# Norm roots by square root and reciprocal instead of logarithm and exponential, and an earlier place for two scalings of the final norm

## The reference

```python
def rmsnorm(x, g):
    xf = x.astype(F32)
    y = xf * lax.rsqrt(jnp.mean(xf * xf, axis=-1, keepdims=True) + EPS)
    return (y * g.astype(F32)).astype(x.dtype)
...
hs = modulate(rmsnorm(xs, norm2_g[l]), m_lat[3], m_lat[4])
xs = xs + m_lat[5] * swiglu(hs, w_ffn_in[l], w_ffn_out[l])
...
y_sample = rmsnorm(xs, final_g)
```

## Time and profile before

| | us |
|---|---|
| median of three runs | 2845.01 |
| profiled execution, its own time | 2845.1 |
| its span | 2843.3 |
| TensorE matmuls busy in the span | 2721.0 (96%) |
| VectorE busy | 1798.9 (63%) |
| ScalarE busy | 884.6 (31%) |
| GpSimd busy | 871.4 (31%) |

### The profile page before, as it was taken

How to read it: one execution, slowest core, us unless ns; L and a number is a source line. 1 busy time by engine, 2 the same in 40 slices (tenths; PEclk the granted TensorE clock), 3 DMA queues, 4 the chain that set the end, 5 groups by cost and what they waited for, 6 DMA issues and landing times. The chain is left out here.

```text
span 2843.3 us, 41885 instructions
## 1 busy us (share of the span) xinstructions
PE 2721.0 (96%) x16344; PEld 2595.5 (91%) x16344; DVE 1798.9 (63%) x2662; ACT 884.6 (31%) x1454; POOL 871.4 (31%) x392
## 2 busy tenths in 40 slices
PE   7998888999999999999999998899999999999998
PEld 5997777999999999999899997559999999999997
DVE  6798986755666666666658614545466666666665
ACT  4213666251122222221542231542512222222214
POOL 0673123422222222222412121434322222222223
PEclk9999999999999999999999999999999999999999
DMA  6543101500111111110335434323101111111102
GB/s 251 182 149 97 18 21 42 204 30 31 45 44 44 44 44 44 44 44 30 124 116 185 169 122 178 130 82 139 45 30 45 44 44 44 44 44 44 44 30 82
DMA packets 64072, 227.29 MB, mean 80 GB/s; under 512 B 8080, under 2 KB 18768, under 8 KB 58576
## 3 DMA queue, kind: packets, MB, share of 16 engines
q1 hardware_dynamic: 62368, 225.12, 22.8%
q10 hardware_dynamic: 1584, 0.51, 0.1%
HBM read 191.52 MB, written 29.88 MB: 78 GB/s over the span
## 5 line engine op out<-in xcount | busy, mean ns | idle before, releaser
L1538 DVE SCALAR_TENSOR_TENSOR x<-ps,mod,x 128x384 f32<-128x384 f32 (+2 forms) x944 | 493.6, 541 | 397.2 <-PE ps L222 397.2
L220 PE MATMUL ps<-hh,wi_hi 128*128 128x384 f32 x2112 | 708.6, 336 | 8.2 <-ACT hid L1132 4.5
L222 PE MATMUL ps<-hh,wi_lo 128*128 128x384 f32 x2112 | 706.2, 334 | 0.0
L221 PE MATMUL ps<-hl,wi_hi 128*128 128x384 f32 x2112 | 706.1, 334 | 0.0
L1294 POOL TENSOR_TENSOR wi_lo<-raw_in,wi_hi 128x1024 fp32r<-128x1024 f32 x80 | 197.7, 2471 | 1016.8 <-ACT wi_hi L1113 1016.8
L220 PEld LDWEIGHTS ps<-hh,wi_hi 128*128 128x128 f32 x2112 | 396.9, 188 | 10.9 <-ACT hid L1132 5.2
L221 PEld LDWEIGHTS ps<-hl,wi_hi 128*128 128x128 f32 x2112 | 397.1, 188 | 0.8
L222 PEld LDWEIGHTS ps<-hh,wi_lo 128*128 128x128 f32 x2112 | 396.9, 188 | 0.0
L220 PE MATMUL ps<-fac_hi,wo_hi 128*128 128x384 f32 x656 | 221.0, 337 | 4.0 <-DVE x L1538 3.2
L1113 ACT ACTIVATE wi_hi<-raw_in 128x1024 fp32r<-128x1024 f32 x80 | 84.7, 1059 | 444.2 <-PE ps L222 444.2
L222 PE MATMUL ps<-fac_hi,wo_lo 128*128 128x384 f32 x656 | 219.9, 335 | 0.0
(11 more groups left out here) (325 smaller groups left out, 5679.6 us busy)
## 6 DMA issues: line engine op xcount, KB each, us to landing
raw_in<-in_w_ffn_in_dram SPq DMA_DIRECT2D x80, 512.0 KB, 3.6
wmt<-in_w_mod_t_dram SPq DMA_DIRECT2D x56, 512.0 KB, 3.6
wo_raw<-in_w_ffn_out_dram SPq DMA_DIRECT2D x22, 1024.0 KB, 4.8
gla_spill<-turn SPq DMA_DIRECT2D x22, 576.0 KB, 3.7
oraw<-in_w_in_odd_dram SPq DMA_DIRECT2D x24, 512.0 KB, 5.2
wmt_odd<-in_w_mod_t_dram SPq DMA_DIRECT2D x24, 512.0 KB, 4.3
x<-in_x_dram SPq DMA_DIRECT2D x8, 1152.0 KB, 9.9
wm<-in_w_mod_dram SPq DMA_DIRECT2D x16, 512.0 KB, 11.8
```

Source lines behind the costliest of these rows:

```text
L220: pe.matmul(acc, w_hi, in_hi, start=first, stop=False, skip_group_check=resumed)
L221: pe.matmul(acc, w_hi, in_lo, start=False, stop=False, skip_group_check=resumed)
L222: return pe.matmul(acc, w_lo, in_hi, start=False, stop=last, skip_group_check=resumed)
L1538: last = dve.scalar_tensor_tensor(out=x[:, ft, cols], in0=ps[:, bank, loc], scalar=mod[:, layer, GATE2 * KT + ft, v:v + 1], in1=x[:, ft, c ...
```

## The change

`logarithm` and `power` go. In their place `root` first runs `warm`, an activation of one column with the square root as its function, that waits for nothing and whose result (in `silu_c`) nobody reads; then `square_root` with the same bank, bias and scale as the logarithm had, which posts `rooting`. The reciprocal of `stat` is made by VectorE in `invert`, at the head of the third's first `scale` or `scale_final`: it waits for `rooting`, takes the reciprocal of 128x384 in place, posts `rooted`, and waits for its own post. TensorE's waits for `logged` become waits for `rooting`. This holds for the three thirds of all four seams, twelve roots. The very first norm of the kernel keeps its logarithm and exponential.

In the final norm `root` of third 1 stands where its `logarithm` stood, with the reciprocal on VectorE ahead of the third's scalings. Six `scale_final` of third 0 instead of four stand ahead of the last gate; the other two come behind `plain_low(5)` and behind the first two adds of third 1.

```diff
         def root(self, act, c, bank):
-            self.logarithm(act, c, bank)
-            self.power(act, c)
-
-        def logarithm(self, act, c, bank):
+            self.warm(act, 3 * (self.n - 1) + c)
+            self.square_root(act, c, bank)
+
+        def square_root(self, act, c, bank):
             act.wait_ge(self.averaged, c + 1)
-            act.activation(self.stat[:, c], bank, ACT.Ln, bias=eps[:], scale=1.0 / D).then_inc(self.logged, 1)
-
-        def power(self, act, c):
-            act.wait_ge(self.logged, c + 1)
-            act.activation(self.stat[:, c], self.stat[:, c], ACT.Exp, scale=-0.5).then_inc(self.rooted, 1)
+            act.activation(self.stat[:, c], bank, ACT.Sqrt, bias=eps[:], scale=1.0 / D).then_inc(self.rooting, 1)
+
+        def warm(self, act, j):
+
+            act.activation(silu_c[:, j // 2, j % 2:j % 2 + 1], ones[:, 0:1], ACT.Sqrt)
+
+        def invert(self, dve, c):
+            dve.wait_ge(self.rooting, c + 1)
+            dve.reciprocal(self.stat[:, c], self.stat[:, c]).then_inc(self.rooted, 1)
+            dve.wait_ge(self.rooted, c + 1)
 
         def scale(self, dve, c, kk):
             if kk == 0:
-                dve.wait_ge(self.rooted, c + 1)
+                self.invert(dve, c)
...
         def scale_final(self, dve, c, kk):
             if kk == 0:
-                dve.wait_ge(self.rooted, c + 1)
+                self.invert(dve, c)
...
-                tail.logarithm(act, 1, end_bank[1])
+                tail.root(act, 1, end_bank[1])
                 for ft in range(6, KT):
                     square_final(2, ft)
-                tail.power(act, 1)
                 tail.root(act, 2, end_bank[2])
...
-                for kk in range(4):
+                for kk in range(6):
                     tail.scale_final(dve, 0, kk)
                 gate(L, 5, 1, 2, 11)
                 plain_low(5)
-                plain_add(1, range(0, 4))
-                for kk in range(4, KT):
-                    tail.scale_final(dve, 0, kk)
-                    plain_add(1, range(kk, kk + 1))
+                tail.scale_final(dve, 0, 6)
+                plain_add(1, range(0, 2))
+                tail.scale_final(dve, 0, 7)
+                plain_add(1, range(2, KT))
                 plain_add(2)
```

More of the change, by code:

```diff
@@ L235, in __init__ @@
             self.squared, self.summed, self.averaged = sem("squared"), sem("summed"), sem("averaged")
-            self.logged, self.rooted = sem("logged"), sem("rooted")
+            self.rooting, self.rooted = sem("rooting"), sem("rooted")
             self.scaled, self.high, self.low = sem("scaled"), sem("high"), sem("low")
@@ L613, in first_pair @@
                     if c == 0:
-                        pe.wait_ge(self.norm.logged, 2)
+                        pe.wait_ge(self.norm.rooting, 2)
                     for m in range(2):
@@ L619, in first_pair @@
                         if c == 2 and m == 1:
-                            pe.wait_ge(self.norm.logged, 3)
+                            pe.wait_ge(self.norm.rooting, 3)
                         block(m, c)
@@ L1476, in _ @@
                 pe.wait_ge(win_low, 2)
-                pe.wait_ge(norm.logged, 1)
+                pe.wait_ge(norm.rooting, 1)
                 pe.wait_ge(taken, place[LAST, 1] + 1)
@@ L1484, in _ @@
                 pe.wait_ge(win_low, 4)
-                pe.wait_ge(norm.logged, 2)
+                pe.wait_ge(norm.rooting, 2)
                 pe.wait_ge(taken, place[LAST, 2] + 1)
@@ L1505, in _ @@
                     hidden(L, n, order=last_blocks)
-                pe.wait_ge(tail.logged, 1)
+                pe.wait_ge(tail.rooting, 1)
                 contract(1)
@@ L2155, in opening @@
             rows_done, rows_out, mod_done, modulated = sem("rows_done"), sem("rows_out"), sem("mod_done"), sem("modulated")
-            squared, summed, averaged, logged, rooted = (sem("squared"), sem("summed"), sem("averaged"), sem("logged"),
+            squared, summed, averaged, logged, rooted = (sem("squared"), sem("summed"), sem("averaged"), sem("rooting"),
                                                          sem("rooted"))
```

## The result

The changed kernel takes 2851.18 us at the median of 15 runs (2846.55 to 2855.51), against 2845.12 us for 15 runs of the kernel before on the same chip. The ratio, from all these runs, is 1.0017 with a 95% interval of 1.0010 to 1.0024: 4.8 us slower, between 2.8 and 6.8 (the two medians by themselves lie 6.1 us apart). The prediction was 2848.8, a sum of +3.8. The slowdown itself is outside the noise; whether it is more or less than 0.2% the interval doesn't tell.

What follows compares the result with a forecast made beforehand. TensorE's matmuls bound the kernel (96% of the span), so only its waits and the tail count. Mid seams +1.8, end of layer 0 -0.2, final norm +2.2 gave +3.8 us: 2848.8 us, range 2842.5 to 2854.5.

Steps and rivals of the forecast that it cites:

- the likeliest case alone: Whole kernel: with a reciprocal of 2.2 to 2.66 us, the time spans 2846.5 to 2850.5 us.
- The reciprocal: On VectorE, 384 columns: taken as 2.45 us, between 2.36 and 2.64 extrapolated from rows of one and nine columns.
- second rival: The reciprocal takes 3.2 us in the same chains: +10.5 us, 2855.6, slower; chance 0.26 with all reciprocals above 2.66.
- the first: First rival: the reciprocal streams in 0.55 us, -7.5 us in all, 2837.6; chance 0.15 with other unseen gains.
- The root in its place: Each root, ScalarE free to first scaling: 0.73 us longer with a table load, 0.57 shorter without.
- fourth rival: Square root's table does not stay; squares, copies or high parts force loads: some +8 us, 2853; chance 0.06.
- Mid seams: Both mid seams: TensorE's restart at the second gate moves 0.89 us later in each, +1.8 us together.
- the wait at third 0's last parts: Mid seams: a new TensorE wait of 0.3 us, absorbed in the 0.44 it waited at the first gate.
- third rival: Mid seams take up the 0.9 and only the tail pays: 2847.1 us, no change; chance within the forecast's 0.53.
- End of layer 0: VectorE's add comes 0.31 us later, TensorE's 0.5 us wait for GpSimd's split goes: -0.2 us in sum.
- Final norm: Third 1 scaled 0.2 us earlier, third 2's reciprocal in VectorE's list between scalings adds 2.4: +2.2 us.
- 9R - 18.3: Whole kernel's change in us, with R the reciprocal's time: nothing at 2.03, +5.5 at 2.64.

Runs made afterwards that it cites:

- e4: The change with the reciprocal reading 64 columns of ones instead of 384 and the square root scaled by a constant; 0.9976 of the kernel before.
- e5: The change with only third 2 of the final norm back on logarithm and exponential, scaling order kept; 1.0006 of the kernel before.
- e8: The change with one Abs_reciprocal_sqrt activation replacing square root and reciprocal, and no warm activation; 2836.35 us, 0.9970 of the kernel before.
- e9: The kernel before with eight one-column ScalarE copies, results unread, ahead of root 2 in each mid seam; 1.0002 of the kernel before.
- e12: The kernel of e9 executed once more, against the kernel before; 2848.57 us in one run.

## Why the prediction came out right

The verdict it gave, no change within 0.2% and leaning slower, holds by the ratio, with 3.8 us predicted and 4.8 [2.8, 6.8] measured; the interval reaches past 0.2%. The median of 2851.18 lies in the stated range and above the 2850.5 that the likeliest case alone was to reach. Step by step:

- **The reciprocal**: 2.45 predicted, 2.55 measured, inside the middle bounds 2.36 and 2.64. Nine columns against one gave the right slope (5.75 and 6.5 ns per column around 6.25) although 384 is forty times as far. The Trainium skill, "VectorE: DVE Perf Modes", section "First, the fixed hardware budget", has a repeat count of 8 for it, from which the prediction estimated 3.2 us; the trace has 2.55, and the measurement decides. With it the second rival falls, and with e4 in hand the first.
- **The root in its place**: 0.84 longer with a load (5.13 - 4.29 to the first scaling, and 4.61 - 3.77 for third 2), which is 2.55 - 1.72 = 0.83. The loads are those that were counted, so the fourth rival is out.
- **Mid seams**: +0.89 each predicted, 3 x 2.55 - 6.46 = +1.2 with the measured reciprocal; +1.39 and +0.89 measured. In layer 0 one step was wrong: the wait at third 0's last parts was to be absorbed in the first gate's. With two more behind it (at 597.30 and 597.96), it delays TensorE's own sum for third 1 (598.83 - 581.62 = 17.21 us behind the mark, before 596.31 - 579.87 = 16.44), and ScalarE, which used to spend that time on a load, now stands 0.18 us before the square root for it (the first row of ScalarE's fence above). The delay passes on through the root: 0.84 - 0.47 + 0.18 + 0.84 = 1.39, the four terms being root 0, root 1 without a load, this wait and root 2. In layer 1 the predicted 0.89 came out by luck. There the first scaling of third 0 meets an add of GpSimd, in the kernel before and in the change:

```profile
2007.89 1.01 POOL L263 TENSOR_TENSOR stat_mid<-stat_mid,sq_mid 128x384 f32<-128x384 f32 x1
2008.00 1.05 DVE L292 SCALAR_TENSOR_TENSOR hl_f<-x,amod,stat_mid 128x128 f32<-128x128 f32 x1 [4.32 <-ACT stat_mid L285]
...
2011.50 1.02 POOL L263 TENSOR_TENSOR stat_mid<-stat_mid,sq_mid 128x384 f32<-128x384 f32 x1
2012.15 0.53 DVE L297 SCALAR_TENSOR_TENSOR hl_f<-x,amod,stat_mid 128x128 f32<-128x128 f32 x1
```

In layer 0, where no add of GpSimd runs beside it, that scaling lasts 0.35 in both kernels. In layer 1 it lasts 1.05 before and 0.53 in the change, where it starts later against the add. That takes up 0.52 of root 0's delay, third 1 is scaled 21.56 us behind the mark instead of 21.52, and the 0.89 is in the main root 2: 0.84 - 0.52 - 0.47 + 0.20 + 0.84 = 0.89, the 0.20 being ScalarE's wait for the sum there. That the add is what stretches the scaling is read from the times alone; no run tried it. The third rival, that the seams absorb the delay, is out for the sum of both, though layer 1 absorbs a part.

- **End of layer 0**: the add's wait grew by 0.33 (0.31 predicted), and the split's wait went. -0.60 measured for -0.2: the gain was undersized, since it was priced at the wait's idle time alone. From TensorE's two matmuls with ones ahead of the split's wait to the second start behind it are 1421.13 - 1419.52 = 1.61 us before and 1423.71 - 1422.89 = 0.82 after, 0.79 less, where 0.52 is idle time.
- **Final norm**: +2.44 for +2.2, and 2 x 2.55 - 2.7 = 2.4 by its own formula. Third 1's scaling comes 0.14 earlier (0.2 predicted), the scalings meet the gate within 0.02 us, and the reciprocal in VectorE's list costs what it lasts. e5 shows that this root is all of it.

With 2.55 the formula 9R - 18.3 gives +4.7; the stages add up to +4.1. The end of layer 0 (0.5 too high) and the second mid seam (0.3 too high) outweigh the first (0.2 too low). That the forecast of +3.8 lies closer to 4.1 than this is luck: a reciprocal taken 0.1 too short lowered the sum by 0.9. What the prediction did not see is that a version with the same eight loads and no reciprocal was there to be had. The Trainium skill, "ScalarE: Activation LUTs", section "What it computes", advises, because of accuracy, VectorE's reciprocal and a `Sqrt` activation in place of the `Rsqrt` function, which was not tried here; the change has these two in the other order. e8's function is another one, and in these chains it is some 13 us ahead of the change's pair by the two ratios (1.0017 [1.0010, 1.0024] and 0.9970 [0.9958, 0.9982]). Times say nothing of how exact either is.

## What to carry to other kernels

Swapping a table load for an operation on another engine is priced at each place by itself: here one edit in twelve roots gained where the old load stood in the way of a later activation, lost 0.8 us where it stood in the chain, and lost the operation's whole length where the old work had been hidden behind the very engine that got the new one. Price an unseen size of an operation from two sizes of the same operation, not from a copy of the right shape: the copy would have given 0.55 us for 2.55. And where two steps compute one function, look for a single activation first.

## What was not expected of the hardware

- VectorE's reciprocal costs 6.25 ns per column (553 ns for 64 columns, 2553 for 384), four and a half times a copy of that shape (557).
- One activation of `Abs_reciprocal_sqrt` over 128x384 lasts 0.58 us, as the logarithm did, and needs no more loads than the square root: eight in twelve roots, none under squares or high parts.
- Behind one and the same wait of 2.14 us, in two executions of one kernel, the granted clock over the next 6 us was 0.73 (e9) and 1.00 (e12). Behind all waits of 2.1 to 2.3 us in the table above, over all kernels, it was lower in 15 of 42; behind 1.4 us it stayed at 1.00 in all six.
- A lower clock cost 1.6 us where nothing came behind it to take it up, and next to nothing where TensorE had a wait for another engine ahead (the add and the split at the end of layer 0).
- A VectorE scaling of 128x128 that lasts 0.35 us alone lasted 1.05 when it started 0.11 us behind the start of a GpSimd add of 1.01 us.
